# Mask and row maximum of attention in one VectorE instruction per head, and split ranks in the router

## What is computed

```python
# layer 0, selected and window branches: softmax over causal scores
s_s = einsum('bqghd,bgqkd->bqghk', qg, k_sel) * scale
p_s = masked_softmax(s_s, valid)
s_w = einsum('bqghd,bkgd->bqghk', qg, kb) * scale
p_w = masked_softmax(s_w, wmask)
...
# layer 1: window of 128 with a sink
s = where(mask, einsum('bqghd,bkgd->bqghk', qg, kb) * scale, -inf)
m = maximum(max(s, axis=-1), sink)
p = exp(s - m[..., None])
den = sum(p, axis=-1) + exp(sink - m)
o = einsum('bqghk,bkgd->bqghd', p, vb) / den[..., None]
...
# mixture: top-1 group, top-2 experts within it
g_idx = argmax(grp_logits)
top_l, top_j = top_k(within, 2)
wts = softmax(top_l) * g_w[:, None]
y = zeros.at[tok].add(expert(x[tok]) * w)
```

## Time and profile before

| what | value |
|---|---|
| median of 3 runs | 1203.84 us (1203.0 to 1207.72) |
| the profiled execution | 1201.92 us, span 1200.1 us, granted clock 0.904 |
| PE busy | 896.3 us (75%) |
| DVE busy | 340.9 us (28%), 881 instructions |
| ACT busy | 188.6 us (16%) |
| DMA | 441.84 MB, mean 368 GB/s over the span |
| chain that ended last | DMA 55%, PE 34%, DVE 5%, ACT 2% |

### The profile page before, as it was taken

One profiled execution on the slowest core, in us unless ns is written; L12 is line 12 of the kernel. 1 busy time (PEld: TensorE's weight loads), 2 busy tenths in 40 slices (PEclk: granted clock), 3 DMA queues, 4 the chain that ended last, 5 costly groups with the idle time before them and its releaser, 6 DMA issues.

```text
span 1200.1 us, 28078 instructions
## 1 busy us (share of the span) xinstructions
PE 896.3 (75%) x12538; PEld 639.1 (53%) x12538; DVE 340.9 (28%) x881; ACT 188.6 (16%) x473; POOL 28.5 (2%) x34
## 2 busy tenths in 40 slices
PE   7999999787675757576758989777767676565665
PEld 6766767564443535454435566655545353444453
DVE  2475545122120202020204563421212121121111
ACT  4233422110000100000003342101100000000000
POOL 2220000000000000000000000000000000000000
PEclk9999999999888988887988999989979788988788
DMA  9954136999999999999999641999999999999996
GB/s 378 427 202 176 71 141 242 425 392 428 428 429 428 428 428 428 428 429 428 429 429 428 274 168 70 389 400 426 428 429 429 429 429 428 429 428 428 428 429 264
DMA packets 31868, 441.84 MB, mean 368 GB/s; under 512 B 3664, under 2 KB 3792, under 8 KB 5328
## 3 DMA queue, kind: packets, MB, share of 16 engines
q1 hardware_dynamic: 31536, 441.05, 87.5%
q10 hardware_dynamic: 288, 0.15, 0.0%
HBM read 440.14 MB, written 1.05 MB: 368 GB/s over the span
## 4 chain that ended last, share of the span: by engine, by line
DMA 55%; PE 34%; DVE 5%; ACT 2%; issue 2%; SPq 1%; DVEq 0%; ACTq 0%
DMA side<-weights 43%; DMA ring<-weights 12%; PE PS L480 10%; PE PS L876 7%; PE PS L866 4%; PE PS L886 1%; PE PS L611 1%; PE PS L517 1%; PE PS L846 1%; PE PS L779 1%; PE PS L490 1%; DVE side L1291 1%; PE PS L552 1%; SPq L315 1%; ACT side L1099 1%
## 5 line engine op out<-in xcount | busy, mean ns | idle before, releaser
L866 PE MATMUL PS<-ring,probT 128*32 128x128 f32 x5120 | 175.2, 297 | 75.6 <-DMA ring<-weights 68.7
L866 PEld LDWEIGHTS PS<-ring,probT 128*32 128x32 f32 x5120 | 155.0, 120 | 93.6 <-DMA ring<-weights 80.5
L866 PE MATMUL PS<-side,probT 128*32 128x128 f32 x3072 | 118.2, 318 | 85.0 <-DMA side<-weights 82.1
L866 PEld LDWEIGHTS PS<-side,probT 128*32 128x32 f32 x3072 | 102.6, 129 | 108.1 <-DMA side<-weights 101.9
L480 PE MATMUL PS<-ring,side 128*128 128x512 f32 (+1 forms) x320 | 133.8, 573 | 2.3 <-ACT side L998 1.4
L1291 DVE TENSOR_TENSOR scr<-scr,PS 128x128 f32<-128x128 f32 x64 | 18.5, 288 | 401.0 <-ACT scr L1218 401.0
L876 PE MATMUL PS<-side,scr 128*32 128x256 f32 x1024 | 86.2, 495 | 33.6 <-DMA side<-weights 29.3
L1774 DVE COPY probT<-PS 32x256 f32<-32x256 f32 x128 | 54.3, 424 | 200.5 <-PE PS L876 199.6
L480 PEld LDWEIGHTS PS<-ring,side 128*128 128x128 f32 x320 | 59.7, 191 | 64.3 <-issue 63.4
L876 PE MATMUL PS<-ring,scr 128*32 128x256 f32 x1024 | 73.2, 428 | 23.9 <-DMA ring<-weights 11.9
L1222 ACT ACTIVATE probT<-PS 32x256 f32<-32x256 f32 x128 | 47.7, 373 | 267.6 <-PE PS L876 266.9
(11 more groups left out here) (243 smaller groups left out, 705.7 us busy)
## 6 DMA issues: line engine op xcount, KB each, us to landing
ring<-weights SPq DMA_DIRECT2D x127, 2048.0 KB, 34.5
side<-weights SPq DMA_DIRECT2D x80, 2048.0 KB, 27.2
ring<-weights SPq DMA_DIRECT2D x4, 512.0 KB, 8.6
xn<-xT_in SPq DMA_DIRECT2D x2, 512.0 KB, 5.4
x<-x_in SPq DMA_DIRECT2D x2, 512.0 KB, 8.7
out<-x SPq DMA_DIRECT2D x2, 512.0 KB, 2.6
TB<-table SPq DMA_DIRECT2D x1, 909.5 KB, 16.6
SM<-small SPq DMA_DIRECT2D x1, 732.0 KB, 17.9
```

Of the source, the lines that this page charges most:

```text
L866: mm = pe.matmul(PS[f * CAP:(f + 1) * CAP, b, up * P:(up + 1) * P], gatherT[:, k, tok], w[:, k, f * P:(f + 1) * P], start=(k == 0), stop=( ...
```

## The change

In `front` the add over all heads and the maximum over all heads are replaced by one fused instruction for each head, which writes the masked scores and the head's maximum. The signal `masked` is given by the last of them. In the router the first half's triangle product goes to bank 5 and signals `ranked` of its own; the second half's waits for a second count; rank and pick are made for one half, then for the other.

```diff
@@ PE, router
-                pe.matmul(PS[:, 7, 0:32], tb("tri"), m[:, 0, :], start=True, stop=True)
-                pe.matmul(PS[:, 7, 32:64], tb("ones"), m[:, 0, :], start=False, stop=False, skip_group_check=True)
+                pe.matmul(PS[:, 5, 0:32], tb("tri"), m[:, 0, :], start=True, stop=True).then_inc(ranked, 1)
+                pe.matmul(PS[:, 7, 32:64], tb("ones"), m[:, 0, :], start=True, stop=False, skip_group_check=True)
                 pe.matmul(PS[:, 7, 64:96], tb("ones"), m[:, 0, :], start=False, stop=False, skip_group_check=True)
                 keep_running(2)
                 pe.wait_ge(chosen, 2 * layer + 2)
@@ DVE, front
                 mask = mask[:, P:2 * P] if t == 0 else mask
-                tt(pr, banks(0, 2).rearrange("p (h c) -> p h c", h=n), mid(mask, n), ALU.add).then_inc(masked, 1)
+                rm = s("rmax")[:, 8 * b:8 * b + n]
+                sc = banks(0, 2).rearrange("p (h c) -> p h c", h=n)
+                for h in range(n):
+                    ins = dve.tensor_tensor_reduce(pr[:, h, :], sc[:, h, :], mask, 1.0, 3.0 * NEG, ALU.add, ALU.max,
+                                                   rm[:, h:h + 1])
+                ins.then_inc(masked, 1)
                 dve.wait_ge(masked, u + 1)
-                rm = s("rmax")[:, 8 * b:8 * b + n]
-                link(dve.tensor_reduce(rm, pr, AX.X, ALU.max))
@@ DVE, router
                 dve.wait_ge(chosen, 2 * layer + 2)
-                dve.wait_ge(ranked, layer + 1)
                 for t in range(TT):
-                    ins = dve.scalar_tensor_tensor(rank[:, t, :], PS[:, 7, t * 32:(t + 1) * 32], 1.0, rt[:, 0, t, :],
-                                                   ALU.add, ALU.mult)
-                link(ins)
-                one_hots(0, build)
+                    dve.wait_ge(ranked, 2 * layer + t + 1)
+                    link(dve.scalar_tensor_tensor(rank[:, t, :], PS[:, 7 if t else 5, t * 32:(t + 1) * 32], 1.0,
+                                                  rt[:, 0, t, :], ALU.add, ALU.mult))
+                    ins = tt(pick[:, t, :].rearrange("p (e c) -> p e c", e=QE), last(rank[:, t, 0:QE], CAP),
+                             mid(tb("iota"), QE), ALU.is_equal)
+                ins.then_inc(m_onehot, 1)
+                dve.wait_ge(m_onehot, build)
```

## The result

| kernel | median | range | ratio to the kernel before, 95% |
|---|---|---|---|
| before, 5 runs beside it | 1203.03 us | 1202.67 to 1207.72 | |
| changed, 5 runs | 1192.84 us | 1189.23 to 1196.12 | 0.9911 [0.9884, 0.9938] |

I had forecast 1201.6, 2.2 us less than before, in a range from 1198.4 to 1207.0. The change took 10.2 us off the median, outside the range on the fast side. Three later comparisons of the same two kernels gave 0.9930, 0.9941 and 0.9936, so the first was at the lucky end; over all four, 23 runs of the changed kernel, the means differ by 8.3 us.

What follows compares the result with a forecast made beforehand. The kernel was taken as a fixed DMA time plus two attention stages. Terms 0 + 1.53 + 0 + 0 + 0.63 + 0.1 = 2.2 us saved gave 1203.84 - 2.2 = 1201.6 us, range 1198.4 to 1207.0.

Steps and rivals of the forecast that it cites:

- What bounds the kernel: Whole kernel: a fixed DMA time plus two attention stages; savings on an attention stage's chain move all behind by as much.
- The price of a pair: Attention masks: fused instruction plus accumulator read, with 0.10 us for the read, costs 0.30 us at 128 columns, 0.44 at 256.
- T8: Mask and maximum of an attention unit with 8 heads: 2.50 us against 2.51 before; 1.70 with a free read.
- T4: Mask and maximum of an attention unit with 4 heads: 1.88 us against 2.51 before; 1.47 with a free read.
- u1: Attention unit of layer 0 with 8 heads, its mask on the chain: gain 0.
- the smaller of 3G and G + 0.90: Layer 0's out-projection: three units gain G (0.63) each, capped by PE's 0.90 us of idle time; 1.53 us earlier.
- u8 with u9: Two attention units of layer 1: the first's gain goes into PE's new wait; together 2 x (1.86 - T4), here nothing.
- u6: Attention unit of layer 1 with 8 heads: gain 0; over 0.46 us, PE's idle time behind it, would not count.
- u10: Attention unit of layer 1: gain 0.63 us, with the exponents, copies and products behind it all shifting.
- The router: Ranks and picks behind PE's sums: 0.24 us less in each layer, counted as nothing in layer 0, 0.1 in layer 1.
- The third: Rival for the fused instructions: the accumulator read is nearly free, 5.3 us faster, 1198.6; chance 0.10.
- the first rival: Rival for the fused instructions: pairs do not overlap, each read waits for its instruction; 3.8 us slower, 1207.6; chance 0.25.

Runs made afterwards that it cites:

- four_heads: Kernel before with the fused mask and maximum only in attention units of 4 heads, router as before: 0.9939 [0.9914, 0.9965] of the kernel before.
- front_only: Kernel before with the fused mask and maximum in all attention units, router as before: 0.9952 [0.9936, 0.9969] of the kernel before.

## Why the prediction was wrong

- **What bounds the kernel: right in kind.** The stream of loads is full in the quads, and saved attention time moved all behind it. What I left out is the scatter of the stages: the same code of layer 0's quads took from 392.8 to 396.5 us in six profiles.
- **The price of a pair: the step that failed.** "I take 0.10, the row of the same kind of read" put 0.30 and 0.44 us on a pair; 0.21 and 0.345 were measured. ScalarE's read, the row I took, had no second activation to run beside: the next one there starts at 180.78, behind the read. VectorE's starts together with the next fused instruction and adds nothing. The lower bound that I had worked out, a free read, was the truth: T8 1.81 (bound 1.70), T4 1.50 (1.47), the gain per unit 0.70 and 1.01 instead of 0 and 0.63. A row of the same engine (0.08 us, the next instruction behind it) stood in the earlier trace rows beside the one I took from another engine.
- **The Trainium skill.** "VectorE: DVE Perf Modes", section "Rules for kernel authors", says not to fuse chained operations for speed, since the pipeline empties after each. The runs here disagree for this instruction: one follows the other after 0.21 us though each lasts 0.29, and even with linked pairs a unit of 4 heads takes 1.87 us against the 2.51 of two long instructions (one of 8 heads 2.67).
- **u1: right, nothing,** for another reason than forecast. It did get 0.70 us shorter, and the second half's sum stood where it would without it (89.18 us in `four_heads`, 89.05 in `front_only`). What took up the 0.70 us is open.
- **Layer 0, "the smaller of 3G and G + 0.90": wrong.** 3G was had, 3.1 us, and with the true G the cap would still have said 1.9. The reason is in the execution that I read. PE ran without a gap from the scores of u5 to the turned outputs, but those scores took 2.92 us, mostly at half clock:

```profile
152.09 2.92 PE L528 MATMUL PS<-side 128*128 128x256 f32 x8
```

  In the second profile of the kernel before they took 1.89, and PE waited:

```profile
150.97 1.89 PE L528 MATMUL PS<-side 128*128 128x256 f32 x8
154.46 1.09 PE L585 MATMUL PS<-TB,xn 128*128 128x128 f32 x8 [1.60 <-DVE xn L1291]
```

  In the first profile VectorE's operation that the turned outputs need had ended just then, too:

```profile
153.65 1.23 DVE L1291 TENSOR_TENSOR xn<-scr,side 128x1024 f32<-128x1024 f32 x1
```

  153.65 + 1.23 is 154.88, and PE began at 154.93. So VectorE set PE's time there, u3's and u4's gains both came through it, and the "busy" PE was only as slow as it could afford to be. The chain of the earlier trace rows had said as much: from u3's mask at 142.44 to the copy that ends at 159.40 it runs through VectorE and ScalarE alone, and PE, which I took for the cap, isn't on it.
- **Layer 1, u8 with u9:** the new wait exists (0.72 us), and 2 x (1.86 - 1.50) = 0.72 by my own rule would have been near: 0.85 were measured where u9's scores ran at full clock (4.49 to 3.64 us from u9's scores to u10's). But three of the changed kernel's four profiles have them mostly at half clock, and there it is 4.72, 5.43 and 4.65 us, 0.2 to 0.9 more than 4.49. (The kernel before has 4.76 in its second profile, its scores of u9 at half clock too.) The worst of them:

```profile
690.71 3.78 PE L528 MATMUL PS<-side 128*128 128x256 f32 x8 [0.57 <-DVE st L1519]
```

  I had no term for that in the sum. u6 gave 0.44, the idle time behind it as I had it; I had forecast nothing only because of T8. u10 gave its 1.0.
- **The router: wrong by its size.** PE's chain got 0.31 us shorter, near the 0.24 counted. Layer 0 "I cost it at nothing: the DMA engines already run full", and layer 1 at 0.1. My 5 us window with 429 GB/s ended before the gap, which lies behind 205 us. The condition that I named for it, a load issued after its forerunner has ended, was the wrong one: the `m_pick` load was issued at 205.44 and 759.70, its forerunner landed only at 208.45 and 763.55, and there was a gap all the same. The changed router closed gaps of 0.7 us on average, by bytes. Why they were longer than the 0.31 us by which the chain moved is open.
- **The sum.** With what was measured: 3.1 + 0.4 + 0.8 + 1.4 = 5.7 us with u9's scores at half clock as in most profiles, 6.7 with them at full clock, against 8.3 (its four comparisons: 10.7, 8.4, 7.1, 7.7 by the ratios). The router's 1.4 in it is by the missing bytes; by PE's chain it is 0.6. Some 2 to 3 us have no place; the intervals of the comparisons are about 3 us to either side each, so this is at the edge of what can be told. It may be in how PE's half-clock stretches fall, and the runs don't settle it.
- **Rivals.** The third (nearly free read, 5.3 us, chance 0.10) had the right price; its sum was still too small. It counted 0.81 for u1, which gave nothing, but kept the cap in layer 0 (1.94 instead of 3.1) and the small router. For the same reasons "even the best bound stays under that", under 6 us, was wrong. In the first rival the sum crosses zero where a pair costs 0.08 more, not 0.07.

## What to carry to other kernels

Price an unseen instruction from rows of its own engine, and let the cheap bound have a fair chance: here the read of a result cost nothing between two instructions, since the next one started beside it. Before calling an engine the limit of a stage, see at which clock it ran there and what its inputs' last writer did: work at half clock hid a wait here, and a cap was read from it that wasn't there. The chain of waits had not passed through that engine. To ask whether a stream of loads has slack, take windows right behind each load whose issue depends on the changed code, 1 us wide, and two profiles of the same kernel, not one.

## What the hardware did that I had not expected

- A fused add and maximum per head with 128 columns follows its forerunner after 0.21 us, nearly as fast as plain adds (0.198), with its accumulator's read of 0.08 us inside.
- PE's granted clock goes from the higher to the lower of its two levels for stretches of some microseconds, at places that differ from execution to execution: the scores of u9 took 1.99 us in one execution and 3.00 to 3.78 in others of the changed kernel (mean granted clock 1.00 against 0.50 to 0.65), and a last down-projection 1.93 or 3.64. Where PE waits anyway this costs nothing, else up to 1.7 us (90.74 against 89.06 in the first stage of the table).
- The fused form seems to move one of these stretches. The scores of u9 ran at a mean granted clock of 0.50 to 0.68 in 7 of the 8 profiles that have the fused form in u8 and no padding, linking or idle products, and in 1 of the other 10. The scores of u5, in layer 0, ran at 0.59 to 0.76 in 4 of 6 profiles with the two long instructions there, and at 1.00 in all 12 with the fused form. At u5 PE waited anyway, at u9 it costs about 1 us of the 1.8. No kernel was made to test this, and why it is so is open.
- Two idle products ahead of a down-projection held the clock at its full level (1.00) there in both layers of both profiles that have them. The gain in time was below what six runs tell.
